# Crossed array quadrants and a VectorE mask in the triangular inverse of an RWKV-7 layer (one Trainium2 core)

## What is computed

```
def step(s, inp):
    r_t, w_t, k_t, v_t, kk_t, a_t = inp
    sa = jnp.einsum('bhij,bhj->bhi', s, -kk_t)
    s = (s * w_t[:, :, None, :]
         + sa[..., None] * (kk_t * a_t)[:, :, None, :]
         + v_t[..., None] * k_t[:, :, None, :])
    return s, jnp.einsum('bhij,bhj->bhi', s, r_t)
...
xs = tuple(jnp.swapaxes(t, 0, 1) for t in (r, decay, k, v, kk, a))
s_fin, ys = lax.scan(step, s0, xs, reverse=reverse)
```

## Time and profile before

| what | value |
| --- | --- |
| median of 3 runs | 5157.78 us (5154.59 to 5157.93) |
| profiled execution | 5157.03 us, its span 5155.2 us |
| PE busy | 4144.5 us (80%) |
| DVE busy | 3534.7 us (69%) |
| POOL busy | 1785.0 us (35%) |
| ACT busy | 1567.6 us (30%) |
| the six turns of `rwkv_pairs` | from about 364 to about 1330 us of the span |

### The profile page before, as it was taken

One profiled execution on the slowest core, in us unless ns is written; L12 is line 12 of the kernel. 1 busy time (PEld: TensorE's weight loads), 2 busy tenths in 40 slices (PEclk: granted clock), 3 DMA queues, 4 the chain that ended last, 5 costly groups with the idle time before them and its releaser, 6 DMA issues. The chain is left out here.

```text
span 5155.2 us, 82317 instructions
## 1 busy us (share of the span) xinstructions
PE 4144.5 (80%) x30538; PEld 3338.1 (65%) x30538; DVE 3534.7 (69%) x7014; ACT 1567.6 (30%) x2840; POOL 1785.0 (35%) x1341
## 2 busy tenths in 40 slices
PE   6768666876676659999999938877936899999994
PEld 1336544555376549999999925435924799999994
DVE  3223454445259859999999953423886799999997
ACT  1122222232121753333333311001248333333332
POOL 0011221122024116666666620001420456666654
PEclk8879788978898879999999969988979899999997
DMA  9420000000110279999999921211006999999995
GB/s 356 170 79 2 17 17 16 3 16 3 71 74 1 65 221 402 397 406 405 402 400 406 388 94 49 77 70 74 2 1 178 358 403 398 406 403 400 406 402 207
DMA packets 402998, 1062.47 MB, mean 206 GB/s; under 512 B 37015, under 2 KB 179607, under 8 KB 399512
## 3 DMA queue, kind: packets, MB, share of 16 engines
q1 hardware_dynamic: 249880, 517.18, 27.0%
q0 software_dynamic: 147456, 536.94, 26.5%
q10 hardware_dynamic: 5440, 5.24, 0.3%
HBM read 997.92 MB, written 61.31 MB: 205 GB/s over the span
## 5 line engine op out<-in xcount | busy, mean ns | idle before, releaser
L648 PE MATMUL bank<-h_parts,u_parts 128*128 128x384 f32 x6144 | 1116.2, 336 | 100.2 <-DVE u_parts L723 100.2
L648 PEld LDWEIGHTS bank<-h_parts,u_parts 128*128 128x128 f32 x6144 | 1082.5, 188 | 120.0 <-issue 100.5
L658 PE MATMUL bank<-v_parts,gg_parts 128*128 128x512 f32 x4608 | 1095.7, 391 | 0.0
L620 POOL DMA_INDIRECT u_rows<-in_u_rows,rows_idx x512 | 697.7, 1363 | 1086.7 <-DVE dots L727 662.3
L658 PEld LDWEIGHTS bank<-v_parts,gg_parts 128*128 128x128 f32 x4608 | 861.2, 188 | 170.5
L733 DVE SCALAR_TENSOR_TENSOR rows_y<-v_rows,row_scale,rows_y 128x1024 f32<-128x1024 f32 x512 | 660.9, 1292 | 28.9 <-DMA v_rows<-in_peer_v,rows_idx 14.5
L626 POOL DMA_INDIRECT v_rows<-in_peer_v,rows_idx x512 | 609.1, 1190 | 168.7 <-issue 147.8
L727 DVE CUSTOM_DVE_ANT_0 u_rows<-u_rows,rows_h 128x1024 f32<-128x1024 f32 x512 | 622.0, 1215 | 0.0
L723 DVE TENSOR_TENSOR u_parts<-hT,u_parts 128x1024 fp32r<-128x1024 f32 x260 | 316.6, 1218 | 70.0 <-ACT u_parts L696 42.2
L692 ACT ACTIVATE ge<-bank 128x384 f32<-128x384 f32 x256 | 126.1, 493 | 675.0 <-PE bank L648 586.0
L327 PE MATMUL bank<-hT,wq 128*128 128x128 f32 x2560 | 310.5, 275 | 4.2 <-PEq L60 4.2
(11 more groups left out here) (303 smaller groups left out, 5459.2 us busy)
## 6 DMA issues: line engine op xcount, KB each, us to landing
hT<-in_peer_u SPq DMA_DIRECT2D x260, 512.0 KB
v_in<-in_peer_v SPq DMA_DIRECT2D x256, 512.0 KB
w_modt<-in_w_mod SPq DMA_DIRECT2D x24, 2048.0 KB, 15.5
gates<-gates_sb SPq DMA_DIRECT2D x6, 8192.0 KB, 30.4
g_in<-gates SPq DMA_DIRECT2D x256, 192.0 KB
wq<-in_peer_wq SPq DMA_DIRECT2D x32, 512.0 KB, 12.9
w_hy<-in_hy_w_in SPq DMA_DIRECT2D x9, 1536.0 KB, 6.3
w_rkv<-in_w_rkv SPq DMA_DIRECT2D x6, 1536.0 KB, 6.7
```

The source lines that it names most:

```text
L620: pool.indirect_dma_start(ug[n % GR][:, :], None, m.i["u_rows"], bass.IndirectOffsetOnAxis(ap=R.idx[:, n % 2, n // 2:n // 2 + 1], axis=0)) ...
L648: mm = pe.matmul(m.bank[j % 2][:, 0:TD], us[:, j % 2, a, k, :], hs[:, b, k, :], start=(k == 0 and i == 0), stop=(k == KD - 1 and i == 2))
L658: mm = pe.matmul(yb[t][c][:, :], gs[:, j, a, t * P:(t + 1) * P], vs[:, j % 2, b, c * BANK:(c + 1) * BANK], start=(first and i == 0), stop= ...
```

## The change

1. **GpSimd's loop over the 25 units and the buffers `LM` go.** `first` multiplies the unmasked `G[:, t, :, 0, :]` by `X`. VectorE puts the level's mask on the product while it copies it from PSUM to `T1`; ScalarE's copy goes. The masks of levels 1 to 5 are transposed in the constants.
2. **Crossed quadrants.** `first` and `turned` read partitions b and write partitions 1 - b (quadrants (0, 64) and (64, 0)). So `X` holds the two chunks with their places exchanged, and `XT` and `T1` too; `second` stays in (0, 0) and (64, 64).
3. **A new order.** `second(u)` is split in halves. TensorE alternates a block of `first(n)` with the second half of `second(n - 2)`, and one of `turned(n - 3)` with the first half of `second(n - 1)`. The loop has one more round.
4. **One more product per tile before the loop,** `rk_swap`: a unit matrix by `G`, 256 columns wide, in the crossed quadrants, into bank 5. VectorE reads `tm[:, 0]` from it.
5. **Behind the loop** `value_z` and the first product with the state write partitions 1 - r, and the product of `XT` and `Zs` reads them and writes r.

```diff
@@ GpSimd @@
-                    for n in range(UNITS):
...
-                        pool.tensor_tensor(hd(LM[:, n % LM_RING]), hd(G[:, t, :, 0, :]), lm[:, lv].unsqueeze(2).broadcast_to(quads), ALU.mult).then_inc(s["rk_lm"], 1)
@@ TensorE @@
+                        for b in range(2):
+                            mm = pe.matmul(m.bank[5][rows(1 - b), 0:4 * CH].rearrange("p (a n) -> p a n", a=4), eye[rows(b), :], G[rows(b), t, :, 0, :], start=True, stop=True,
+                                           tile_position=(CH * b, CH * (1 - b)))
+                        mm.then_inc(s["rk_swap"], 1)
...
                     def first(n, b, q):
-                        return pe.matmul(m.bank[6 + n % 2][rows(b), CH * q:CH * q + CH], LM[rows(b), n % LM_RING, q, :], X[rows(b), n % TT, q, :], start=True, stop=True,
-                                         tile_position=(CH * b, CH * b))
+                        return pe.matmul(m.bank[6 + n % 2][rows(1 - b), CH * q:CH * q + CH], G[rows(b), n % TT, q, 0, :], X[rows(b), n % TT, q, :], start=True, stop=True,
+                                         tile_position=(CH * b, CH * (1 - b)))
...
-                    for n in range(UNITS + 1):
-                        u, v = n - 1, n - 2
+                    for n in range(UNITS + 2):
+                        u, v = n - 2, n - 3
                         if n < UNITS:
-                            pe.wait_ge(s["rk_lm"], n + 1)
...
+                        for q in range(4):
+                            if n < UNITS:
+                                first(n, 0, q)
+                            if u >= 0:
+                                mm = second(u, q % 2, 2 + q // 2)
+                                if q == 3:
+                                    mm.then_inc(s["rk_t2t"], 1)
+                            if n < UNITS:
+                                mm = first(n, 1, q)
...
+                        u = n - 1
+                        if 0 <= u < UNITS:
                             pe.wait_ge(s["rk_t1sb"], u + 1)
...
+                        for q in range(4):
+                            if 0 <= v < UNITS - TT:
+                                turned(v, 0, q)
+                            if 0 <= u < UNITS:
+                                second(u, q % 2, q // 2)
+                            if 0 <= v < UNITS - TT:
+                                mm = turned(v, 1, q)
@@ ScalarE @@
-                            act.activation(T1[:, n % 3].rearrange("p a b -> p (a b)"), m.bank[6 + n % 2][:, 0:4 * CH], ACT.Copy).then_inc(s["rk_t1sb"], 1)
@@ VectorE @@
-                        dve.wait_ge(s["rk_gsb2"], t + 1)
-                        dve.tensor_tensor(hd(tm[:, 0]), hd(G[:, t, :, 0, :]), lm[:, 0].unsqueeze(2).broadcast_to(quads), ALU.mult)
+                        dve.wait_ge(s["rk_swap"], t + 1)
+                        dve.tensor_tensor(hd(tm[:, 0]), hd(m.bank[5][:, 0:4 * CH].rearrange("p (a n) -> p a n", a=4)), lm[:, 0].unsqueeze(2).broadcast_to(quads), ALU.mult)
...
-                    for n in range(UNITS):
+                    for u in range(UNITS + 2):
+                        if u < UNITS:
+                            dve.wait_ge(s["rk_t1"], u + 1)
+                            if u >= 3:
+                                dve.wait_ge(s["rk_t2t"], u - 2)
+                            dve.tensor_tensor(hd(T1[:, u % 3]), hd(m.bank[6 + u % 2][:, 0:4 * CH].rearrange("p (a n) -> p a n", a=4)),
+                                              lm[:, 1 + u // TT].unsqueeze(2).broadcast_to(quads), ALU.mult).then_inc(s["rk_t1sb"], 1)
+                        n = u - 2
```

More of the change, by code:

```diff
@@ L1221, in _ @@
                                 pe.wait_ge(s["rk_t1sb"], n - 1)
-                            for q in range(4):
-                                for b in range(2):
-                                    mm = first(n, b, q)
-                            mm.then_inc(s["rk_t1"], 1)
-                        if u >= 0:
+                        for q in range(4):
[7 more added lines that the diff above has]
+                                mm = first(n, 1, q)
+                                if q == 3:
+                                    mm.then_inc(s["rk_t1"], 1)
+                        u = n - 1
+                        if 0 <= u < UNITS:
                             pe.wait_ge(s["rk_t1sb"], u + 1)
@@ L1231, in _ @@
                                 pe.wait_ge(s["rk_xt"], TT + u - 1)
-                            for q in range(4):
-                                for b in range(2):
-                                    mm = second(u, b, q)
-                            mm.then_inc(s["rk_t2t"], 1)
                         if 0 <= v < UNITS - TT:
@@ L1239, in _ @@
                                 pe.wait_ge(s["rk_xsb"], v - 1)
-                            for q in range(4):
-                                for b in range(2):
-                                    mm = turned(v, b, q)
-                            mm.then_inc(s["rk_xtr"], 1)
+                        for q in range(4):
[5 more added lines that the diff above has]
+                                mm = turned(v, 1, q)
+                                if q == 3:
+                                    mm.then_inc(s["rk_xtr"], 1)
                     pe.wait_ge(s["rk_xt"], TT + UNITS)
@@ L1257, in value_z @@
                         d, t = held(n, r)
-                        return pe.matmul(zu[rows(r), h, 0:CH], G[rows(r), t, 2 * d + h, 2, :], vt[rows(r), t, rows(h)], start=True, stop=False,
-                                         tile_position=(CH * r, CH * r), skip_group_check=True)
+                        return pe.matmul(zu[rows(1 - r), h, 0:CH], G[rows(r), t, 2 * d + h, 2, :], vt[rows(r), t, rows(h)], start=True, stop=False,
+                                         tile_position=(CH * r, CH * (1 - r)), skip_group_check=True)
                     def value_y(n, r, h):
@@ L1288, in _ @@
                                 d, t = held(n, r)
-                                pe.matmul(zu[rows(r), h, 0:CH], AR[rows(h), d, t, 0, rows(r)], st[rows(h), g, d, :], start=False, stop=True,
-                                          tile_position=(CH * h, CH * r), skip_group_check=True)
+                                pe.matmul(zu[rows(1 - r), h, 0:CH], AR[rows(h), d, t, 0, rows(r)], st[rows(h), g, d, :], start=False, stop=True,
+                                          tile_position=(CH * h, CH * (1 - r)), skip_group_check=True)
                         if n >= 1:
@@ L1307, in _ @@
                                 d, t = held(n, r)
-                                mm = pe.matmul(ob[rows(r), 0, CH + CH * h:2 * CH + CH * h], XT[rows(r), t, 2 * d + h, :], Zs[rows(r), n % 2, rows(h)], start=False, stop=True,
-                                               tile_position=(CH * r, CH * r), skip_group_check=True)
+                                mm = pe.matmul(ob[rows(r), 0, CH + CH * h:2 * CH + CH * h], XT[rows(1 - r), t, 2 * d + h, :], Zs[rows(1 - r), n % 2, rows(h)], start=False, stop=True,
+                                               tile_position=(CH * (1 - r), CH * r), skip_group_check=True)
                         mm.then_inc(s["rk_umm"], 1)
@@ L1369, in _ @@
                         act.activation(BKt[:, d, j, 4], m.bank[2 * n + 1][:, 0:P], ACT.Copy).then_inc(s["rk_bksb"], 1)
[L1370 to L1376 removed]
+                    for n in range(UNITS):
+                        v = n - 3
                         if 0 <= v < UNITS - TT:
@@ L1578, in scan_masks @@
     level = lambda n, d: (s // (2 * n) == t // (2 * n)) & ((late(t, n) & ~late(s, n)) if d == 0 else (late(s, n) & ~late(t, n)))
-    lmask = np.stack([np.stack([level(2 ** k, d) for d in range(2)], 1) for k in range(LEVELS)] + [np.stack([level(1, 1 - d) for d in range(2)], 1)], 1)
+    lmask = np.stack([np.stack([level(2 ** k, d if k == 0 else 1 - d) for d in range(2)], 1) for k in range(LEVELS)] + [np.stack([level(1, 1 - d) for d in range(2)], 1)], 1)
     return gmask, lmask
```

20 lines of the change are left out of this document (5 added, 15 removed).

## The result

| | kernel before | changed kernel |
| --- | --- | --- |
| median | 5157.85 us (5154.59 to 5164.58, 6 runs) | 5175.26 us (5170.43 to 5182.97, 6 runs) |
| profiled execution | 5157.03 us, span 5155.2 us | 5175.17 us, span 5173.4 us |
| ratio | 1 | 1.0024, 95% interval 1.0014 to 1.0035 |

The forecast was 5158 us, no change, with a range of 5137 to 5176. The time is inside the range by 0.7 us and 17 us above the forecast: the change makes the kernel slower by 0.24%, which is the outcome that had 17%. The two medians of this table alone would give 1.0034; the six runs of the kernel before were low ones. In its 64 later runs the medians were 5163 to 5166 us, and against those 5175 is 1.0019 to 1.0023, so the ratio of 1.0024 is the better figure.

The account below looks back on a forecast made before the run. The loop was taken to run at the pace of PE's instruction fetch, with PE's work the second limit, 6% behind. Terms -1.4 + 1.2 + 1.4 = +1.2 us on the profiled 5157.0 gave 5158 us, range 5137 to 5176.

Parts of the forecast that it names:

- the outcome that had 17%: Whole kernel slower by more than about 0.2% (10 us), made up of two rivals with 11% and 6%.
- The fetch as the limit of the loop: In the loop, instruction fetch, 3.85 us or more per block of 256 instructions, becomes alone the limit; +1.4 us.
- the two turns that should stay: Loops of turns 1 and 6, already nearly throughout at the fetch's pace (31.50 and 32.17 us): no change.
- the other four: Loops of the remaining turns, 121.15 us together, could rise by between 0 and +2.8 us; taken as +1.4.
- GpSimd's silence: Ahead of the loop, L1448 on VectorE no longer slowed by GpSimd working beside it: -1.4 us, or 0.
- The entry: Up to the loop's first block boundary, swap product against faster first units: +0.2 us per turn, +1.2 in all.
- harmless: In the loop, VectorE busy 0.84 of 0.93 us per unit has little room, but the fetch limit makes that harmless.
- Rival E: In the loop, quadrants don't overlap in this order: unit stays 1.40 us, time 5157; no chance of its own.
- Behind the loop, "0, between -1 and +1": In the steps after the loop, products change quadrants, not number or order: 0 us, between -1 and +1.
- rival B: At loop entries and in steps behind loops, the clock is kept more often: -10 to -25 us, 5135 to 5148; 15%.
- Rival C: In the loop, PE now idles and its clock falls to 1.2 GHz: +9 to +36 us; 11%.

Follow-up runs that it names:

- tiny: Changed kernel with four more matmuls of two columns per unit in units 2 to 24, 16 instructions more per unit; 5202.95 us.
- merged: Changed kernel with half of the loop's matmuls, each twice as wide, some products wrong, for timing alone; 5120.58 us.
- mask_only: Kernel before with VectorE's mask in place of GpSimd's and ScalarE's copy, old quadrants and order, no swap product; 5162.49 us, ratio 0.9999 to the kernel before.
- early: Changed kernel with the first two units' `first` and masked copies moved ahead of the last tile's first level; 5159.61 us, ratio 0.9991 to the kernel before.

## Why the prediction was right or wrong, step by step

- **The fetch as the limit of the loop: right.** PE's work per unit fell to 0.99 us (1.02 forecast), the gaps came in nearly every block and are put down to "issue" (0.4 to 1.3 us, mostly under the 1 us forecast), the packets stayed at 6 in 23 us, and `tiny` and `merged` show that the count of instructions decides. The 48 blocks took 186.9 us, +2.1 where +1.4 stood: the two turns that should stay fell by 2.0, the other four rose by 4.0, over their bound of 2.8. For the kernel before the claim went too far: in turn 5 PE was busy 29.61 of 29.72 us, and turns 2, 3 and 5 have no gap. There PE's own work was the limit, with the fetch close behind.
- **GpSimd's silence: right.** From the first matmul of `tables` to the first `first`, the six turns take 93.1 us where they took 95.0: -1.9, forecast -1.4. L1447, which was L1448, takes 424 ns at the median against 494:

```profile
L1447 DVE TENSOR_TENSOR XT<-eye,tm x30: 424/424/427, 398.6 to 1273.5; 128x256 f32<-128x256 f32 x30
```

- **The entry: the cause was half of it, and the term too small.** From the first `first` to the first `second` the six turns take 14.5 us where they took 10.3, +4.2 against the +1.2 that the sum had up to the first block boundary. I reckoned with two more matmuls ahead of the transpose (their 0.4 us on VectorE came true) and with DVE busy by 0.84 of 0.93 us per unit, "harmless" under the fetch. In the loop it is. (L1445 also ran ahead of the 0.84 us wait, not inside it.) At the entry and the exit there is no fetch to hide behind: there the masked copy stands behind the last tile's operations (5.1 us in six turns against ScalarE's copy), and at the end it lengthens the chain (2.3 us). The change as a whole still came close to the +1.2 us forecast for this stretch (+1.3 in the profiled run, +5.1 and +1.6 in the two others), since the crossed order gains some 4 us there by itself. That the sum met the forecast is luck: its terms were off in both directions.
- **Rival E, quadrants that don't overlap: refuted,** by the 0.99 us. The rule in part 3 of the page "TensorE: Matmul & The Clock Gate" of the Trainium skill, that a load overlaps only matmuls of another row group, would by my reading have kept 1.40 us; the trace doesn't follow it here.
- **Behind the loop, "0, between -1 and +1": the step that failed.** It was +20.1 us in the profiled run, +11.1 and +17.2 in the other two; 4.2 of the 20.1 are turn 6, a fall of the clock that the other two don't have. I had looked at the products there (same number, same order, and turn 2 bears that out) and not at the clock with which the loop hands over to them. The rows were at hand: the earlier trace rows has 64.60 us at clock 1.00 and 70.90 at 0.88 for the same work. I used them in rival B alone, for a gain (its lower end is 5133, not 5135).
- **Rival C, the clock falls inside the loop: right in the cause, wrong in the place.** PE does idle and the clock does fall for it, but in the blocks it stayed at 1.00 behind the entry. It falls just behind the loop. The place matters. In `tiny` the clock did fall inside two of the six loops, for 3.4 us each, with PE busy all through:

```profile
1142.60:1146.00 3.40, 3.40 (x110) 3.40 (x101) 0.75 (x2) 0.77 (x2) 0.00 (x0) 0.51 0.02 5
```

This is turn 5, whose stretch took 58.18 us, no more than turns 4 and 6 (58.44 and 58.37): beneath the fetch the low clock cost nothing to be seen. In the steps nothing hides it.
- **The size of what a trace can show.** The profile of before happened to have the shortest steps of all 14 (373.4 us; `mask_only` with the same loop had 380.5). So the +20 us is in part chance, and so was the profiled 5157.0 us that the forecast started from. The timed ratios, 1.0024 and 1.0020, are 12 and 10 us; tables and loops (+3 in the mean) and steps (389.6 against 376.9) account for them, less some 3 us in the rest of the program, which lies between 4462 and 4470 us in all 14 traces. Even so, the forecast's "no change" was wrong by just over its own bound.

## What to carry to other kernels

Before speeding up a dense run of small matmuls, count its instructions: if a block of 256 already takes as long as its fetch, less work per instruction changes nothing, and only fewer, wider instructions help. Idle time on TensorE that "costs nothing" can be paid for by the next stretch, through its clock; look at the granted clock behind the place that is changed. A copy that moves to another engine is hidden in the steady loop, so look for its price at the entry and the exit, where it stands behind that engine's other work.

## What the runs showed of the hardware

- Eight blocks of 256 instructions take 30.6 to 32.3 us with 144 us of PE's work in the 48, and 29.7 to 32.2 us with 180. Single blocks of the changed kernel take mostly 3.8 or 4.1 us, at the ends 3.5 and 4.4. Why some take longer stays open.
- Two fp32 transposes of 128x128 show one pass each and take 0.37 us to the next product, where eight products of 64x64 with a unit matrix took 0.47 us and eight times the instructions.
- Short idle times of TensorE, 0.4 to 1.7 us at a time, in loops whose granted clock stayed at 1.00 behind the entry (but for two of `tiny`), were followed by a fall within 2 us of the loop's end (just before or behind it) in 18 of 35 cases, and in none of 35 with PE nearly always busy. In the other 17 the fall came as late as before. Which it will be I couldn't tell from the rows ahead.
- Filling 2 us of idle PE ahead of the loop's entry kept the clock at 1.00 there, where it had been 0.51; in the six loops of `early` together it was low for 0.3 us.
